# Gates of a linear recurrent unit in chains of three, half-height products in pairs, and retention in chunks of 256 tokens

## The chip, the cores and the metric

The kernel runs on one core of one Trainium2 chip. The metric is the device time of one execution, in microseconds (us), as the median of repeated runs. The engines are PE (matrix products), DVE, ACT and POOL (elementwise work) and SP, which here only issues transfers. They run in parallel and wait for each other on semaphores.

## What is computed

Two decoder layers on 1024 tokens of width 1024, in float32. The first layer's mixer is retention, the second's a gated linear recurrence (RG-LRU); each is followed by a dense SwiGLU. What the change touches is this:

```python
def step(state, inp):                      # retention, chunk by chunk, 4 heads, dk 256, dv 512
    qi, ki, vi = inp
    scores = jnp.einsum('bhqd,bhkd->bhqk', qi, ki) * intra[None]
    o_inner = jnp.einsum('bhqk,bhkv->bhqv', scores, vi)
    o_cross = jnp.einsum('bhqd,bhdv->bhqv', qi, state) * q_decay[None, :, :, None]
    new_state = state * chunk_decay[None, :, None, None] + jnp.einsum(
        'bhkd,bhkv->bhdv', ki * k_decay[None, :, :, None], vi)
    return new_state, o_inner + o_cross
...
# RG-LRU, width 1536 in 8 blocks of 192
r = jax.nn.sigmoid(jnp.einsum('bsnc,ncd->bsnd', ub, w_r) + b_r).reshape(B, S, LRU_WIDTH)
i = jax.nn.sigmoid(jnp.einsum('bsnc,ncd->bsnd', ub, w_i) + b_i).reshape(B, S, LRU_WIDTH)
log_a = (-LRU_C * jax.nn.softplus(-lam.astype(jnp.float32))) * r.astype(jnp.float32)
a = jnp.exp(log_a)
b = jnp.sqrt(-jnp.expm1(2.0 * log_a)) * (i * u).astype(jnp.float32)
...
y = hs.astype(h.dtype) * jax.nn.gelu(gate)   # hs: the scan of h = a*h + b over the tokens
return y @ w_out
```

The result does not depend on the length of a chunk, as long as the decays are kept.

## The kernel before

Every float32 operand of a product is held as two rounded parts, upper and lower, so a product takes three instructions on PE (helper `three`, lines 770 to 777: upper x upper at L773, the other two at L776 and L777). ACT (or POOL, for weights) makes the upper part, DVE (or POOL) the lower one by a subtraction. The order on each engine is the order of the code of that engine; nothing is scheduled. PSUM has 8 banks of 512 columns. Each use of a bank has a running number, an event; PE counts filled events in `psum_full`, and the engine that reads one last counts it in `psum_free`. `free(e)` makes PE wait until event e - 8, the last user of the same bank, is released, and `psum_free` is one counter, so every earlier event must be released too.

**Retention**, four heads in turn. PE makes q and k (pair 0 and pair 1 in `head` of DVE, which rotates them, L2009 to L2025, and splits them, L2030), the gate branch g, the scores (`SCORES`: for each key block of 128 tokens the queries that see it, in chunks of `CHUNK` = 4 blocks, 512 tokens), the turned keys (L966, L967, by an identity), and the values v. Then come `values(s)` for each of 8 blocks of 128 tokens and `state_sum`, the sum of k times v over the first chunk, in banks 6 and 7; ACT rounds the state (L1500), DVE splits it (L2069), and the later chunk's blocks multiply q with it. `o_turns` turns the gated output for the product with w_out.

**RG-LRU**, four groups of 3 tiles of 128 channels, which are two blocks of 192. Per group PE makes the u branch and the gate branch (`lru_into`, twice 3 tiles of 48 products), the output products of the group before (`lru_outof`), and the gate products (`lru_gates`). There an item is one tile and one half of the tokens, and has two banks, r and i. `MEETS` says which of the three 128-channel blocks of u a tile needs: tile 0 needs 0 and 1, tile 1 all three, tile 2 needs 1 and 2. The block 1 for tiles 0 and 2 is used only in half of its rows; the rest of the weights is zero. Seven blocks times two gates times three instructions are 42 per half.

The chain behind it, per pair of items, is `gate_chain` on ACT and DVE: sigmoid of r (L1777) and i (L1782), u times i on DVE (`gated`, L2405, which releases both banks), tanh (L1791) and exp (L1795) of r, square root (L1801), then on DVE in `scans` two multiplies (L2413, L2417), the scan (L2422) and the product with the other branch (L2429), and at last `y_split` (L2434). ACT loads a table when it goes from sigmoid and tanh to exp, and to the square root, and back. The function `meanwhile` puts adds of output products to the residual (`add`, L1998) between the steps of the last group.

In the last group the gates stand in the middle of the output products of the group before: s = 0 to 3 of the first half of columns, the gates, s = 4 to 7, and then the second half of columns (`lru_outof` with nh = 1, 72 products), whose k = 0 round takes one bank after the other: s = 4 needs the bank that the first half's s = 4 was added from. Behind it comes the last group's own output (`out_by_halves`, 16.3 us for a half), which needs y.

## Time and profile before

| | us |
|---|---|
| median of 3 runs | 2703.74 (2703.36 to 2703.92) |
| the profiled execution | 2702.78 |
| its span in the trace | 2701.0 |
| PE busy | 2672.0 (99%) |
| DVE busy | 1273.9 (47%) |
| ACT busy | 831.3 (31%) |
| POOL busy | 1267.7 (47%) |

The times of single instructions below are from the one profiled execution. A busy time on PE is that of one product from its first column to its last result, and neighbours overlap, so the distance from start to start is what a product takes of PE. Retention lies between 16 and 876 us, the first SwiGLU behind it, RG-LRU between some 1550 and 2027 us, and the second SwiGLU to the end.

### The profile page before, as it was taken

The numbers are of one execution on the slowest core, as the hardware profiler recorded it, in microseconds if no ns is written. First come the engines' busy times: TensorE is split into PE (matmuls) and PEld (weight loads), VectorE is DVE, ScalarE is ACT, GpSimd is POOL, SyncE is SP. The second block draws the span as 40 slices with busy tenths as digits, with TensorE's granted clock in tenths as the row PEclk, the third lists the DMA queues.
The fourth block names the chain that finished last, engine by engine and source line by source line (L and its number), as shares of the span: only waits on it lengthen the run. The fifth ranks groups of instructions, "written<-read, shape, count | busy, mean of one in ns | idle before, by whom it ended". The sixth has DMA issues, their size and how long they took to land.

```text
span 2701.0 us, 35201 instructions
## 1 busy us (share of the span) xinstructions
PE 2672.0 (99%) x12017; PEld 2213.0 (82%) x12017; DVE 1273.9 (47%) x1719; ACT 831.3 (31%) x1388; POOL 1267.7 (47%) x1208
## 2 busy tenths in 40 slices
PE   8999999999999999999999999999999999999998
PEld 6888888888888788888888788888887888888887
DVE  8333322323334854444444447365688444444444
ACT  4120120120124533333333515234365222222224
POOL 4324323323423455655555454363454556655555
PEclk9999999999999999999999999999999999999999
DMA  4101102111111111111121021111111111111212
GB/s 143 44 28 63 44 28 63 47 32 59 48 36 44 51 51 54 47 47 54 53 64 51 27 60 44 36 55 40 44 55 47 55 54 47 47 47 55 69 50 83
DMA packets 173768, 139.29 MB, mean 52 GB/s; under 512 B 9200, under 2 KB 143472, under 8 KB 173680
## 3 DMA queue, kind: packets, MB, share of 16 engines
q1 hardware_dynamic: 171584, 133.46, 16.2%
q10 hardware_dynamic: 2096, 4.62, 0.5%
q8 instruction: 59, 0.97, 0.1%
q14 instruction: 29, 0.24, 0.0%
HBM read 132.81 MB, written 5.24 MB: 51 GB/s over the span
## 4 chain that ended last, share of the span: by engine, by line
PE 95%; DVE 3%; ACT 1%; issue 1%; DMA 0%; SPq 0%; DVEq 0%
PE ps L773 31%; PE ps L777 31%; PE ps L776 31%; DVE f_h_lo L2144 1%; PE ps L1085 0%; PE ps L1009 0%; PE ps L849 0%; PE ps L911 0%; DMA residual<-in_x 0%; DVE gate_buf L2082 0%; DVE f_h_lo L2133 0%; DVE h_sum_a L2133 0%; DVE gate_buf L2222 0%; ACT f_h_hi L1581 0%; DVE h_sum_a L2158 0%
## 5 line engine op out<-in xcount | busy, mean ns | idle before, releaser
L602 POOL TENSOR_TENSOR f_w_lo<-f_raw,f_w_hi 128x512 fp32r<-128x512 f32 x270 | 357.5, 1326 | 449.6 <-ACT f_w_hi L1532 364.6
L773 PE MATMUL ps<-f_h_hi,f_w_hi 128*128 128x512 f32 x1232 | 481.1, 390 | 3.6 <-DVE f_h_lo L2144 2.3
L777 PE MATMUL ps<-f_h_hi,f_w_lo 128*128 128x512 f32 x1232 | 479.5, 389 | 0.0
L776 PE MATMUL ps<-f_h_lo,f_w_hi 128*128 128x512 f32 x1232 | 479.4, 389 | 0.0
L560 POOL TENSOR_TENSOR small<-w_raw 128x1 f32<-128x1 f32 x200 | 59.5, 297 | 804.6 <-PE ps L773 794.1
L2333 DVE TENSOR_TENSOR residual<-ps,residual 128x512 f32<-128x512 f32 x352 | 239.4, 691 | 170.5 <-PE ps L777 170.4
L773 PEld LDWEIGHTS ps<-f_h_hi,f_w_hi 128*128 128x128 f32 x1232 | 231.2, 188 | 57.2 <-issue 4.4
L1532 ACT ACTIVATE f_w_hi<-f_raw 128x512 fp32r<-128x512 f32 x246 | 155.1, 631 | 382.9 <-PE ps L777 382.8
L777 PEld LDWEIGHTS ps<-f_h_hi,f_w_lo 128*128 128x128 f32 x1232 | 231.3, 188 | 48.3
L776 PEld LDWEIGHTS ps<-f_h_lo,f_w_hi 128*128 128x128 f32 x1232 | 231.3, 188 | 47.2
L773 PE MATMUL ps<-f_w_hi,f_act_hi 128*128 128x512 f32 x688 | 267.8, 389 | 0.0
L776 PE MATMUL ps<-f_w_lo,f_act_hi 128*128 128x512 f32 x688 | 267.6, 389 | 0.0
L777 PE MATMUL ps<-f_w_hi,f_act_lo 128*128 128x512 f32 x688 | 267.6, 389 | 0.0
L571 POOL TENSOR_TENSOR w_lo<-w_raw,w_hi 128x512 fp32r<-128x512 f32 x190 | 259.1, 1364 | 15.2
L773 PE MATMUL ps<-h_hi,w_hi 128*128 128x512 f32 x632 | 247.5, 392 | 0.0
L777 PE MATMUL ps<-h_hi,w_lo 128*128 128x512 f32 x632 | 246.0, 389 | 0.0
L776 PE MATMUL ps<-h_lo,w_hi 128*128 128x512 f32 x632 | 246.0, 389 | 0.0
L602 POOL TENSOR_TENSOR f_w_lo<-f_sum,f_w_hi 128x512 fp32r<-128x512 f32 x124 | 180.4, 1455 | 124.1 <-ACT f_w_hi L1532 124.1
L773 PE MATMUL ps<-w_hi,h_hi 128*128 128x512 f32 x528 | 205.7, 390 | 0.4 <-DVE gate_buf L2021 0.4
L776 PE MATMUL ps<-w_lo,h_hi 128*128 128x512 f32 x528 | 205.5, 389 | 0.0
L777 PE MATMUL ps<-w_hi,h_lo 128*128 128x512 f32 x528 | 205.5, 389 | 0.0
L2288 DVE TENSOR_TENSOR gate_buf<-ps,gate_buf 128x512 f32<-128x512 f32 x120 | 82.8, 690 | 235.1 <-PE ps L777 235.0
(305 smaller groups left out, 4643.8 us busy)
## 6 DMA issues: line engine op xcount, KB each, us to landing
f_raw<-in_ffn_w_gu SPq DMA_DIRECT2D x176, 256.0 KB, 3.3
w_raw<-in_ret_w_in SPq DMA_DIRECT2D x96, 256.0 KB, 2.8
f_raw<-in_ffn_w_down SPq DMA_DIRECT2D x88, 256.0 KB, 2.8
w_raw<-in_lru_w_in SPq DMA_DIRECT2D x48, 256.0 KB, 2.9
w_raw<-in_ret_w_out SPq DMA_DIRECT2D x32, 256.0 KB, 2.6
w_raw<-in_lru_w_out SPq DMA_DIRECT2D x24, 256.0 KB, 2.6
residual<-in_x SPq DMA_DIRECT2D x8, 512.0 KB, 7.2
out_y<-residual SPq DMA_DIRECT2D x7, 512.0 KB, 2.6
```

What stands on the lines that cost most here:

```text
L560: nc.gpsimd.tensor_tensor(small[:, 62:63], col, col, ALU.subtract)
L571: nc.gpsimd.tensor_tensor(lo, raw[:, cut], hi.bitcast(F32), ALU.subtract).then_inc(w_ready, 1)
L602: nc.gpsimd.tensor_tensor(lo, src, hi.bitcast(F32), ALU.subtract).then_inc(f_wready, 1)
L773: m = nc.tensor.matmul(o, l_hi, r_hi, start=start, stop=False, skip_group_check=onto)
L776: nc.tensor.matmul(o, l_hi, r_lo, start=False, stop=False, skip_group_check=onto)
L777: return nc.tensor.matmul(o, l_lo, r_hi, start=False, stop=stop, skip_group_check=onto)
L1532: nc.scalar.activation(f_unit(j, last)[0], src, ACT.Copy).then_inc(f_whi, 1)
L2144: TT(H_lo[:, h_cut(form, k)], src[:, t_cut(k)], H_hi[:, h_cut(form, k)].bitcast(F32), ALU.subtract).then_inc(hn_dve, 1)
L2288: TT(t, f_bank(u, p), t, ALU.add).then_inc(f_ev, 1)
L2333: TT(X[:, c], ps[:, b * BANK:(b + 1) * BANK], X[:, c], ALU.add).then_inc(f_ev, 1)
```

## The change

Retention works in four chunks of 256 tokens: per chunk 128 and 256 columns of scores, turned keys for three chunks, and three states, each summed on top of the one before in the same banks (`state_sum(i)`, with waits for the split of the last). The queries of tokens 256 to 511 are copied a second time (`query_tile`), since v takes the place of the first copy.

The gate products run in another order (tile 1 first), and the six of block 1 for tiles 0 and 2 are issued on 64 rows each, in turn. The chain takes three items at a time, with more buffers. In the last group the first three items' chain takes item 3's sigmoids first (`early` = 1), and s = 4 to 7 of the output are made in two pairs.

```diff
-CHUNK = 4
...
-SCORES = [pieces for c in (0, CHUNK) for pieces in ([(c, 512)], [(c + 3, 128), (c + 1, 384)], [(c + 2, 256)])]
...
-MEETS = [(0, 1), (0, 1, 2), (1, 2)]
+CHUNK, N_CHUNKS = 2, 4
...
+SCORES = [(1, P), (0, 2 * P)]
+SCORE_N = 3 * P
...
+GATE_TILES = (1, 0, 2)
...
-        r_buf = (t(0), r3(6), dk[:, 0:512], spare[0])
+        r_buf = (t(0), r3(6), dk[:, 0:512], spare[0], behind[0][:], behind[1][:])
         i_buf = (t(1), spare[1], spare[2])
-        s_buf = (r3(7), t(2))
+        s_buf = (r3(7), t(2), behind[2][:])
...
+                        k_h, k_l = qk_at(1, d, i // 2)
+                        for c in range(CHUNK):
+                            q = (i % 2 * CHUNK + c) * P
+                            cut, o = slice(q, q + P), bank(J_K + i, (d * CHUNK + c) * P, P)
+                            nc.tensor.matmul(o, k_h[:, cut], ident_r[:], start=True, stop=False)
+                            m = nc.tensor.matmul(o, k_l[:, cut], ident_r[:], start=False, stop=True)
+                    m.then_inc(psum_full, 1 if i < N_CHUNKS - 2 else 2)
                 for k in range(KT):
                     cols_unit(16 + k, ub + 16 + k, k, KT, h_hi, h_lo, k * S, J_V, base)
...
+                def state_sum(i):
...
+                            pe.wait_ge(st_ready, 6 * h + 2 * i - 2 + d + 1)
...
-                            cut, v = slice(c * P, (c + 1) * P), slice(c * 512, (c + 1) * 512)
-                            m = three(bank(J_O + 6 + d), k_h[:, cut], k_l[:, cut], a_hi[:, v], a_lo[:, v],
-                                      c == 0, c == CHUNK - 1)
+                            k_h, k_l = k_turned(i, P, (d * CHUNK + c) * P)
+                            b = i * CHUNK + c
+                            v = slice(b * 512, (b + 1) * 512)
+                            m = three(bank(J_O + 6 + d), k_h, k_l, a_hi[:, v], a_lo[:, v],
+                                      i == 0 and c == 0, c == CHUNK - 1, onto=i > 0)
                         m.then_inc(st_full, 1)
-                pe.wait_ge(s_ready, h * len(SCORES) + len(SCORES))
+                pe.wait_ge(s_ready, h * N_CHUNKS + N_CHUNKS)
                 def values(s):
-                    late = s >= CHUNK
...
+                        m.then_inc(psum_full, 1)
+                def from_state(s):
+                    for d in range(2):
+                        pe.wait_ge(st_ready, 6 * h + (s // CHUNK - 1) * 2 + d + 1)
+                        m = three(bank(J_O + s), *query(s, d), *state(d), False, d == 1)
...
+                state_sum(0)
+                for i in (1, 2):
+                    values(2 * i)
+                    values(2 * i + 1)
+                    from_state(2 * i)
+                    from_state(2 * i + 1)
+                    state_sum(i)
+                o_turns(range(4))
+                for s in (6, 7):
                     values(s)
-                state_sum()
-                for s in range(3, SB - 1):
-                    values(s)
-                o_turns(range(4))
-                values(SB - 1)
+                    from_state(s)
                 if last:
...
+                    def halves_meet():
+                        for m_i in range(2):
+                            a_w, a_wl, a_u, a_ul = operands(0, m_i, 1, slice(0, 64))
+                            b_w, b_wl, b_u, b_ul = operands(2, m_i, 1, slice(64, P))
+                            a, b = bank(event(0, m_i)), bank(event(2, m_i))
+                            nc.tensor.matmul(a, a_w, a_u, start=False, stop=False)
+                            nc.tensor.matmul(b, b_w, b_u, start=False, stop=False)
+                            nc.tensor.matmul(a, a_w, a_ul, start=False, stop=False)
+                            nc.tensor.matmul(b, b_w, b_ul, start=False, stop=False)
+                            nc.tensor.matmul(a, a_wl, a_u, start=False, stop=True)
+                            m = nc.tensor.matmul(b, b_wl, b_u, start=False, stop=True)
...
+                        m.then_inc(psum_full, 4)
...
+                    if hf == 0:
+                        pe.wait_ge(u_ready, len(U_PIECES) * g + 2)
+                    meets(0, 0, True, False)
+                    meets(1, 0, True, False)
+                    meets(1, 1, False, False)
+                    pe.wait_ge(u_ready, len(U_PIECES) * g + 3 + hf)
+                    meets(1, 2, False, True)
+                    meets(2, 2, True, False)
+                    halves_meet()
...
-            for first in (0, 4):
+            for first, n in ((0, 4), (4, 2), (6, 2)):
...
-                    for s in range(first, first + 4):
+                    for s in range(first, first + n):
...
-                        .then_inc(qk_rounded, 1)
+                    src = (t(0), t(1), t(2), r3(7))[i % 4]
+                    nc.scalar.activation(qk_at(pair, d, hf)[0], src, ACT.Copy).then_inc(qk_rounded, 1)
+                    if pair == 0 and hf == 0:
+                        nc.scalar.activation(query_tile(d)[0], src[:, 256:512], ACT.Copy).then_inc(q2_rounded, 1)
...
                 def tanh_exp(items):
                     for i in items:
-                        if i >= 2:
-                            act.wait_ge(l_scan, 6 * g + i - 1)
...
+                            act.wait_ge(psum_free, base + e0 + 2 * (GT + early) + 2)
...
-                gates(4)
-                gates(5)
-                tanh_exp((2, 3))
-                roots((2, 3))
-                tanh_exp((4, 5))
-                y_round((2, 3))
-                roots((4, 5))
-                y_round((4, 5))
+                for i in range(GT + early):
+                    gates(i)
+                tanh_exp((0, 1, 2))
+                roots((0, 1, 2))
+                for i in range(GT + early, 2 * GT):
+                    gates(i)
+                tanh_exp((3, 4, 5))
+                y_round((0, 1, 2))
+                roots((3, 4, 5))
+                y_round((3, 4, 5))
...
-                split_state()
-                gate_o((3,))
-                gate_o((4,))
+                gate_o((0, 1))
+                split_state(0)
+                gate_o((2, 3))
+                split_state(1)
                 norm_o(0)
-                gate_o((5, 6))
+                gate_o((4, 5))
+                split_state(2)
                 o_turned_lower(range(4))
-                gate_o((7,))
+                gate_o((6, 7))
                 norm_o(1)
...
                     for j, i in enumerate(items):
                         dve.wait_ge(dve_step, first + j + 1)
-                        step.up(TT(uc[:, cut(i)], uc[:, cut(i)], s_buf[i % 2], ALU.mult))
+                        step.up(TT(uc[:, cut(i)], uc[:, cut(i)], s_buf[i % 3], ALU.mult))
+                    amid()
                     for j, i in enumerate(items):
-                        dve.wait_ge(dve_step, first + j + 3)
-                        tile, hf = i % GT, i // GT
+                        dve.wait_ge(dve_step, first + len(items) + j + 1)
...
                         start = uc[:, tile * S + 511:tile * S + 512] if hf else 0.0
-                        k = nc.vector.tensor_tensor_scan(uc[:, cut(i)], r_buf[i % 4], uc[:, cut(i)], start,
+                        k = nc.vector.tensor_tensor_scan(uc[:, cut(i)], r_buf[i], uc[:, cut(i)], start,
...
                 TS(gc_gate[:, 0:3], gc_gate[:, 21:24], -2.0, None, ALU.mult).then_inc(gc_ready, 1)
-                gated((0, 1))
-                scans((0, 1), amid=lambda: gated((2,)))
-                gated((3,))
-                y_split((0, 1))
-                gated((4, 5))
+                gated(range(GT + early))
+                scans((0, 1, 2), amid=lambda: gated(range(GT + early, 2 * GT)))
+                y_split((0, 1, 2))
                 meanwhile(0, range(4, SB))
-                scans((2, 3))
-                y_split((2, 3))
-                scans((4, 5), lambda: meanwhile(1, range(SB)))
-                y_split((4, 5))
+                scans((3, 4, 5), lambda: meanwhile(1, range(SB)))
+                y_split((3, 4, 5))
             per_turn = 1 + 3 * 3 + 1 + 6 * 2
```

On PE in the last group, behind the products of tile 1 and 2: `h_hi`, `h_lo` are the parts of u, `wri_hi`, `wri_lo` those of the gate weights. Before, in the first half of the tokens:

```order
L773 MATMUL ps<-h_hi,wri_hi 128x512 [waits psum_free]
L776 MATMUL ps<-h_lo,wri_hi 128x512
L777 MATMUL ps<-h_hi,wri_lo 128x512
L773 MATMUL ps<-h_hi,wri_hi 128x512
L776 MATMUL ps<-h_lo,wri_hi 128x512
L777 MATMUL ps<-h_hi,wri_lo 128x512
L773 MATMUL ps<-h_hi,wri_hi 128x512 [waits u_ready,psum_free]
L776 MATMUL ps<-h_lo,wri_hi 128x512
L777 MATMUL ps<-h_hi,wri_lo 128x512
L773 MATMUL ps<-h_hi,wri_hi 128x512
L776 MATMUL ps<-h_lo,wri_hi 128x512
L777 MATMUL ps<-h_hi,wri_lo 128x512
```

After, from the same half, the first twelve of block 1 for tiles 0 and 2:

```order
L1323 MATMUL ps<-h_hi,wri_hi 128x512
L1324 MATMUL ps<-h_hi,wri_hi 128x512
L1325 MATMUL ps<-h_lo,wri_hi 128x512
L1326 MATMUL ps<-h_lo,wri_hi 128x512
L1327 MATMUL ps<-h_hi,wri_lo 128x512
L1328 MATMUL ps<-h_hi,wri_lo 128x512
L1323 MATMUL ps<-h_hi,wri_hi 128x512
L1324 MATMUL ps<-h_hi,wri_hi 128x512
L1325 MATMUL ps<-h_lo,wri_hi 128x512
L1326 MATMUL ps<-h_lo,wri_hi 128x512
L1327 MATMUL ps<-h_hi,wri_lo 128x512
L1328 MATMUL ps<-h_hi,wri_lo 128x512
```

Twelve instructions on 128 rows become twelve that stand alternately on rows 0 to 63 (L1323, L1325, L1327) and 64 to 127, behind all others of the half.

On DVE in the last group, from the first products of y on (`gate_buf` from the scan `uc`) to the next adds to the residual. Before:

```order
L2429 TENSOR_TENSOR gate_buf<-uc,gate_buf 128x512 [waits l_scan] x2
L2405 TENSOR_TENSOR uc<-uc,tmp 128x512 [waits i_sig]
L2434 TENSOR_TENSOR h_lo<-gate_buf,h_hi 128x512 [waits y_rounded] x2
L2405 TENSOR_TENSOR uc<-uc,xn 128x512 [waits i_sig] x2
L1998 TENSOR_TENSOR residual<-ps,residual 128x512 [waits psum_full] x4
```

After, the same stretch; the multiplies and the scans ahead of it are shown too:

```order
L2492 TENSOR_TENSOR uc<-uc,gate_buf 128x512 [waits dve_step]
L2492 TENSOR_TENSOR uc<-uc,tmp 128x512 [waits dve_step]
L2492 TENSOR_TENSOR uc<-uc,lru_gate 128x512 [waits dve_step]
L2480 TENSOR_TENSOR uc<-uc,xn 128x512 [waits i_sig] x2
L2498 SCALAR_TENSOR_TENSOR uc<-tmp,uc 128x512 [waits dve_step]
L2498 SCALAR_TENSOR_TENSOR uc<-gate_buf,uc 128x512 [waits dve_step]
L2498 SCALAR_TENSOR_TENSOR uc<-mask,uc 128x512 [waits dve_step]
L2503 TENSOR_TENSOR gate_buf<-uc,gate_buf 128x512 [waits l_scan] x3
L2508 TENSOR_TENSOR h_lo<-gate_buf,h_hi 128x512 [waits y_rounded] x3
L2065 TENSOR_TENSOR residual<-ps,residual 128x512 [waits psum_full] x4
```

The four adds, which stood behind `y_split` of two items and two `gated`, now stand behind the scans, products and `y_split` of three items.

## Rows read from the trace of the kernel before

**Rows 1.** The page: busy time by engine, and the last chain by engine.
```profile
PE 2672.0 (99%) x12017; PEld 2213.0 (82%) x12017; DVE 1273.9 (47%) x1719; ACT 831.3 (31%) x1388; POOL 1267.7 (47%) x1208
...
PE 95%; DVE 3%; ACT 1%; issue 1%; DMA 0%; SPq 0%; DVEq 0%
```

**Rows 2.** Waits of PE, longest first: total, times, longest, in us.
```profile
PE ps L874 <- DMA scratch<-in_lru_lambda: 9.6, 1, 9.6
```

**Rows 3.** Line 773, last group's gates: count, min/median/max ns, first, last start.
```profile
L773 PE MATMUL ps<-h_hi,wri_hi x28: 389/389/389, 1946.6 to 1965.0; 128*128 128x512 f32 x28
```

**Rows 4.** Timeline of PE, scores of head 0: start us, us, engine.
```profile
109.69 0.39 PE L773 MATMUL ps<-a_hi 128*128 128x512 f32 x1
...
111.22 0.27 PE L777 MATMUL ps<-a_hi,a_lo 128*128 128x128 f32 x1
111.33 0.27 PE L773 MATMUL ps<-a_hi 128*128 128x128 f32 x1
...
112.90 0.28 PE L776 MATMUL ps<-a_lo,a_hi 128*128 128x256 f32 x1
113.02 0.28 PE L777 MATMUL ps<-a_hi,a_lo 128*128 128x256 f32 x1
...
117.32 0.22 PE L966 MATMUL ps<-ident_r,a_hi 128*128 128x128 f32 x1
...
119.06 0.44 PE L773 MATMUL ps<-w_hi,h_hi 128*128 128x512 f32 x1
```

**Rows 5.** Timelines of DVE and of ACT, states and values of head 0.
```profile
158.97 5.37 DVE L2062 SCALAR_TENSOR_TENSOR a_lo<-ps,gam,a_hi 128x512 fp32r<-128x512 f32 x8 [38.28 <-ACT a_hi L1481]
...
169.67 0.60 ACT L1500 ACTIVATE b_hi<-ps 128x512 fp32r<-128x512 f32 x1 [1.94 <-PE ps L777]
...
170.30 0.69 DVE L2069 TENSOR_TENSOR b_lo<-ps,b_hi 128x512 fp32r<-128x512 f32 x1 [1.78 <-ACT b_hi L1500]
```

**Rows 6.** Timeline of DVE: a 256-wide instruction of the scores.
```profile
114.19 0.42 DVE L2047 TENSOR_TENSOR tmp<-ps,mask 128x256 f32<-128x256 f32 x1
```

**Rows 7.** Timelines of DVE and PE ahead of the k pair.
```profile
64.97 0.69 DVE L2009 TENSOR_TENSOR tmp<-ps,gate_buf 128x512 f32<-128x512 f32 x1
...
70.76 0.50 PE L773 MATMUL ps<-w_hi,h_hi 128*128 128x512 f32 x1 [0.38 <-DVE gate_buf L2021]
...
267.82 0.69 DVE L2009 TENSOR_TENSOR tmp<-ps,gate_buf 128x512 f32<-128x512 f32 x1 [1.44 <-PE ps L777]
```

**Rows 8.** Timelines of DVE and ACT ahead of the gates of group 2.
```profile
1852.28 3.07 DVE L1998 TENSOR_TENSOR residual<-ps,residual 128x512 f32<-128x512 f32 x5
...
1858.73 1.28 ACT L1777 ACT_TABLE_LOAD   x1 [3.16 <-DVE gc_gate L2439]
```

**Rows 9.** Timeline of ACT, gate chain of the last group.
```profile
1948.22 1.28 ACT L1777 ACT_TABLE_LOAD   x1 [5.60 <-PE ps L777]
1949.51 0.69 ACT L1777 ACTIVATE tmp<-ps,gc_gate 128x512 f32<-128x512 f32 x1
1950.10 0.68 ACT L1782 ACTIVATE tmp<-ps,gc_gate 128x512 f32<-128x512 f32 x1
...
1956.84 0.73 ACT L1795 ACTIVATE tmp<-tmp,gc_gate 128x512 f32<-128x512 f32 x1
...
1959.50 0.63 ACT L1801 ACTIVATE gate_buf<-gate_buf 128x512 f32<-128x512 f32 x1
```

**Rows 10.** Timeline of PE behind the gates of the last group.
```profile
1967.43 0.50 PE L773 MATMUL ps<-w_hi,a_hi 128*128 128x512 f32 x1 [0.26 <-DVE uc L2405]
...
1977.11 0.39 PE L773 MATMUL ps<-w_hi,a_hi 128*128 128x512 f32 x1
```

**Rows 11.** Timeline of DVE, gate chain of the last group.
```profile
1962.66 1.22 DVE L2422 TENSOR_TENSOR_SCAN uc<-tmp,uc 128x512 f32<-128x512 f32 x1
...
1972.55 2.73 DVE L1998 TENSOR_TENSOR residual<-ps,residual 128x512 f32<-128x512 f32 x4 [1.79 <-PE ps L777]
...
1976.29 1.78 DVE L2413 SCALAR_TENSOR_TENSOR tmp<-xn,tmp 128x512 f32<-128x512 f32 x1
```

More of the change, by code:

```diff
@@ L217, in build @@
               for kb in (123, 127, 131, 135)]
+        behind = [over(kb, f"lru_gate{kb}", 512) for kb in (159, 161, 163)]
         f_hi, f_lo = over(44, "f_w_hi", RING * 512, F32R), over(50, "f_w_lo", RING * 512, F32R)
@@ L1496, in head @@
                                          accum_out=ssq[:, s:s + 1]).then_inc(o_sq, 1)
-                    if s == 2:
-                        for d in range(2):
-                            act.wait_ge(st_full, 2 * h + d + 1)
-                            nc.scalar.activation(state(d)[0], bank(J_O + 6 + d), ACT.Copy).then_inc(st_rounded, 1)
-                    if s == 6:
-                        o_turned_upper(range(4))
                     if s % 4 == 3:
@@ L1506, in head @@
                                              scale=1.0 / DV).then_inc(o_root, 1)
+                    if s in (1, 3, 5):
+                        for d in range(2):
+                            act.wait_ge(st_full, 6 * h + s - 1 + d + 1)
+                            nc.scalar.activation(state(d)[0], bank(J_O + 6 + d), ACT.Copy).then_inc(st_rounded, 1)
+                    if s == 5:
+                        o_turned_upper(range(4))
                 o_turned_upper(range(4, SB))
```

204 lines of the change are left out of this document (102 added, 102 removed).

## The prediction, before the changed kernel ran

> **What bounds the kernel now.** I read the shares of the span first: PE is busy 99% of it, and the chain that ended last runs on PE for 95% [rows 1]. The list of waits then says how little PE waits: the longest is 9.6 us before its first instruction, which this change does not touch [rows 2], and the others are far smaller. So an edit is worth what it takes out of PE's stream of products, minus the waits that it creates. The price of a product comes from start to start, not from its busy time of 389 ns, which overlaps its neighbour: 27 triples start between 1946.6 and 1965.0, 0.681 us a triple, so a **slot** is 0.227 us for 512 columns [rows 3]. Narrow ones are not proportional: 128 columns start 0.11 apart and 256 columns 0.12 [rows 4]. A product of 128 columns should stream in a quarter of the slot, so 0.11 is what the load of its 128x128 weights costs. That floor prices half of this change.
>
> **Scores and turned keys** (each of 4 heads). Before, the 48 score products take 109.69 to 117.32, 7.63 us, and the 16 turns 117.32 to 119.06, 1.74 us or 0.109 each [rows 4]. After, the scores are 24 products of 128 and 24 of 256 columns: 24 x 0.111 + 24 x 0.119 = 5.52 us, and 24 turns are 2.61 us. Gain 9.37 - 8.13 = 1.24 a head, **-5.0 us**. By columns alone it would be 5120 fewer, 2.27 us a head, but the floor of 0.11 takes half.
>
> **States and values.** Before: 28 triples of values and 8 of the state; after: 12 on the diagonal, 12 from a state, 12 for three states. 108 slots both times, so **0**. What is new is three passes PE -> ACT -> DVE -> PE. Nearest rows: the state's copy on ACT takes 0.60, the split on DVE 0.69 and starts 0.03 after it [rows 5]. With the product's end and the two blocks in front on both engines, the second half of state 0 is ready 1.7 us after state_sum(0) ends, and PE has 9 products of values(2), values(3) and 3 of the first half in front, 2.7 us. The later two have 12 slots and the 16 transposes. state_sum(0) now starts after 9 slots instead of 18, at 162.67 + 2.04 = 164.7, and waits for the last of the value splits, which ends at 158.97 + 5.37 = 164.34 [rows 5]. Covered by 0.3 us; were the cover gone, it is 0.3 to 1 us a head. I take 0.
>
> **The extra halves of q.** Two 256-wide splits on DVE (busy 0.42 [rows 6], 0.33 from start to start if they overlap by 0.09 as the 0.69-long adds below do) and two copies on ACT stand before the k pair. In heads 1 to 3 DVE idles 1.44 us there [rows 7], so they are hidden. In head 0 it has a backlog (no idle at 64.97) and PE already waits 0.38 for its result at 70.76 [rows 7]: all of it shows, **+0.7 us**. Retention: -4.3.
>
> **The gate products.** Per half and group 42 products before, all with full slots, half of the rows of 12 of them zeros (tile 0 and tile 2 against the middle block). After, these 12 stand as 6 pairs on rows 0 to 63 and 64 to 127. No row shows fewer than 128 rows. Low bound for a pair: two weight loads, 2 x 0.111 = 0.222; high bound: two slots, 0.454. The halves share no row and no PSUM bank, only the loader, so I take one slot, 0.227: 6 slots less, 1.36 us a half, 2.72 a group. The first and last product of such a block meet full-height ones. If one must be out before the next begins, that is 0.389 - 0.227 = 0.16 at each side, plus one uncovered weight load of 0.11: 0 to 0.9 us a block, I take 0.45.
>
> The Trainium skill (TensorE: Matmul & The Clock Gate, Part 3: Packing small matmuls) says that products on different row groups run side by side, starting 4 ns apart, with 3.07x measured for four; by it a pair is a slot plus 4 ns, the value that I take, and no row here shows it. Against the change speaks the Trainium skill (TensorEngine Tiling (Array Packing), Key Properties): a change of tiling mode drains the engine. By it the low end of 0 for a block would fall away; it does not change the value taken.
>
> Two new waits stand in this stage. (1) The first triple of a group now writes the second item's bank, and needs 3 and 4 of the second adds instead of 1 and 2. In the loop's groups the adds start at 1852.28, 0.6 apart, the third ends at 1854.17, and the gates start at 1854.13 [rows 8]: 0.1 each. (2) Item 0 is now tile 1 and is full only after 24 products. In the last group: 23 slots + 0.39 + 0.1 = 5.7 us after the stage's start T0. Then ACT loads a table, 1.28, and makes two sigmoids, 0.6 apart and 0.69 long [rows 9], and DVE multiplies, 0.69: the banks are free at T0 + 9.1, while PE is there at 8.2 to 8.6. Group 0 has the same order, table load included; in groups 1 and 2 ACT was held until 1858.73 + 1.28 = 1860.0 anyhow [rows 8], T0 + 5.9, and frees at about T0 + 8.0, in time. So group 0 takes 9.15 + 8.16 + 0.45 = 17.75 against 19.05, -1.3; groups 1 and 2 take 0.1 + 16.33 + 0.9 = 17.35, -1.7 each. **-4.7 us**. Behind these groups stand 65 us of input products, so the longer chain is free; it needs item 3 released 28 us after T0, and the sum below puts that at 23.
>
> **The last group** has only 20 blocks of output products behind it, and here I expect the loss. Before, PE begins s=4 of the last turn's second half at 1977.11, T0 + 30.5 [rows 10]; its bank needs the DVE add of s=4, which came at 1972.55 after a wait for PE [rows 11], so free. After, that add stands behind y_split of three items. From T0: second half starts 9.15, item 3 is full 14.85, its sigmoids to 16.1, three tanh to 17.9, table 1.28, three exp (0.73 long) to 21.2, table to 22.5, three roots (0.63 long) to 24.2, table to 25.5, sigmoids of items 4 and 5 to 27.9 [rows 9]. DVE: three STT from 23.3, three multiplies to 26.95, gated(4) to 27.6, gated(5) to 28.7, three scans (1.22 long, 1.14 apart [rows 11]) to 32.1, three multiplies to 34.1, y_split of three to 35.6, the first add to 36.3. DVE has hardly an idle microsecond in it, and single instructions stretch from 0.69 to 1.78 while POOL splits weights [rows 11]; POOL has three units to do there, so + 1.0. PE also waits for item 4 first (27.65 against 25.9), inside the same stretch. PE starts s=4 at T0 + 37.3, 6.8 later than before. The three items' second turn then makes DVE some 1.5 us later at the next norm, of which PE sees perhaps 0.5, since it waits there little. **+7.3 us** instead of -2.7.
>
> **Sum.** -5.0 + 0.7 - 4.7 + 7.3 = -1.7 us. The profiled execution is 2702.78 (span 2701.0 and 1.8 around), so 2701.1 for it; the median of runs is 1.0 above it: 2703.74 - 1.7 = **2702.0 us**.
>
> **Rivals.**
> A, as summed, with ends: blocks at 0 or 0.9 instead of 0.45 (-2.3 / +2.7 in the six that show), stretch by POOL 0 to 3. 2697 to 2706, chance 0.50.
> B, the last chain does not hold PE: the DVE order lets the add through in time, or POOL and ACT are quicker than the rows, and the last group gains like group 0. For it: the change splits PE's last four blocks in two pairs, which takes a wait away (0.26 idle at 1967.43 [rows 10]). Against: the order of DVE puts y_split ahead of the add. -5.0 + 0.7 - 4.7 - 1.3 = -10.3: 2693.4. Chance 0.15.
> C, slower: pairs do not overlap, that is the change doesn't do what it says on PE. Each half then keeps 42 slots and adds 0.45. It decides at the price of a pair: over about 0.38 us. For it: every product in the trace, however narrow, has a slot of its own; against: nothing but the loader is shared. -4.3, groups 0 to 2 + 2.9, the last one 7.3 + 0.8, since item 3 is full that much later: +6.7, 2710.4. Chance 0.20.
> D, between A and B: the stall is there but half as long, because parts of the chain overlap more: -5, 2698.5, chance 0.15.
>
> **How the numbers follow.** A change of this kernel can be told from none at about 0.2%, 5.4 us. Faster by more is B, a part of D, a thin end of A: 0.22. Slower by more is most of C and the end of A: 0.20. The rest, 0.58, is within. The range takes A and D and reaches to C: 2695 to 2710, with the middle of B left out; the likeliest case alone is 2697 to 2706.
>
> **What would show it.** In the profile after: score products of a head in 5.5 us; pairs on the gate stage that start 0.227 apart as pairs (or 0.227 each, which is C); in group 0 a wait of PE for DVE's product of uc at T0 + 9; in the last group a wait of 1 to 2 us for item 4 and one of 5 to 8 us for the residual add before s=4 of the second half, the largest new wait of PE; in head 0 a wait of 1.1 us where 0.38 was. No wait in from_state. If the wait for the residual add is missing, or starts of the two halves of a pair are a slot apart, the prediction is wrong.

## The result, and the profile after

The changed kernel takes **2707.33 us** (median of 20 runs, 2706.36 to 2709.57), the kernel before 2703.61 us on the same chips (20 runs, 2702.88 to 2704.11): a ratio of 1.0014, 95% interval 1.0008 to 1.0021. The time lies inside the range of 2695 to 2710 and within the 0.2% that I called no change, but the sign of the forecast was wrong: -1.7 us was expected and about +3.7 came. The profiled run of the changed kernel is 2706.43 us long (span 2704.6), 3.65 more than the 2702.78 of before. This difference is taken apart below, by where PE stands in both traces.

The page of the changed kernel, busy time by engine and the last chain, beside [rows 1]:

```profile
PE 2665.1 (99%) x12049; PEld 2202.0 (81%) x12049; DVE 1291.4 (48%) x1731; ACT 828.2 (31%) x1400; POOL 1268.2 (47%) x1208
...
PE 90%; DVE 7%; ACT 2%; issue 1%; DMA 0%; SPq 0%; DVEq 0%; ACTq 0%
```

PE has 7 us less to do and yet the kernel is longer, and DVE's share of the last chain has gone from 3% to 7%. PE's list of waits (total, times, longest) names the new holders; the first row answers to [rows 2]:

```profile
PE ps L896 <- DMA scratch<-in_lru_lambda: 9.5, 1, 9.5
PE ps L795 <- DVE residual L2065: 6.1, 2, 6.0
...
PE ps L795 <- DVE uc L2480: 2.9, 1, 2.9
...
PE ps L795 <- DVE gate_buf L2088: 0.4, 1, 0.4
PE ps L795 <- DVE gate_buf L2083: 0.3, 1, 0.3
```

The two long ones are the two that the prediction placed in the last group: 2.9 us for the product on DVE (line 2480) that frees item 4's banks, and 6.0 us for the residual add (line 2065) that stands behind y_split. The timeline of PE around them (start us, length us, engine, line; a bracket is idle time and its releaser), beside [rows 10]:

```profile
1967.19 0.47 PE L795 MATMUL ps<-w_hi,a_hi 128*128 128x512 f32 x1 [2.91 <-DVE uc L2480]
...
1968.35 0.63 PE L798 MATMUL ps<-w_lo,a_hi 128*128 128x512 f32 x1
1968.78 0.63 PE L799 MATMUL ps<-w_hi,a_lo 128*128 128x512 f32 x1
...
1977.75 0.80 PE L795 MATMUL ps<-w_hi,a_hi 128*128 128x512 f32 x1 [5.99 <-DVE residual L2065]
...
1981.71 0.39 PE L795 MATMUL ps<-w_hi,a_hi 128*128 128x512 f32 x1
1981.94 0.39 PE L798 MATMUL ps<-w_lo,a_hi 128*128 128x512 f32 x1
```

Look at the distance between starts. 1968.35 to 1968.78 is 0.43 us and 1981.71 to 1981.94 is 0.23: behind each of the two waits PE runs for a while at half its pace (behind the first one only from its fourth product on). The stretches with the granted clock (length, busy time and count of PE, PEld, DVE, ACT, POOL, then the clock, the DMA share and GB/s) say why:

```profile
1965.00:1975.00 10.00, 4.58 (x12) 3.28 (x12) 10.00 (x10) 6.55 (x10) 7.26 (x6) 0.82 0.25 79
1975.00:1980.00 5.00, 2.25 (x5) 1.82 (x6) 5.00 (x9) 3.91 (x6) 0.00 (x0) 0.50 0.00 2
1980.00:1985.00 5.00, 5.00 (x20) 4.06 (x19) 1.29 (x3) 0.00 (x0) 1.99 (x3) 0.84 0.01 3
1985.00:1990.00 5.00, 5.00 (x24) 4.14 (x23) 1.29 (x2) 0.00 (x0) 1.58 (x4) 1.00 0.15 52
```

The granted clock is 0.50 between 1975 and 1980, that is 1.2 GHz instead of 2.4. From 1977.75 to 1981.71 PE starts 9 products in 3.96 us, where nine slots at full clock are 2.04: **1.9 us** lost after the wait was over. Nothing in the prediction has a price for that, though the trace of the kernel before holds an example. At the norm ahead of RG-LRU, PE waits 2.93 us for DVE, and the granted clock of the next 3.5 us is 0.63 in the mean:

```profile
1545.10 5.11 PE L911 MATMUL ps<-ident,xn 128*128 128x128 f32 x23 [2.93 <-DVE xn L1895]
...
1545.00:1548.50 3.50, 3.33 (x13) 2.51 (x14) 2.32 (x6) 2.86 (x6) 0.00 (x0) 0.63 0.00 0
```

The Trainium skill (TensorE: Matmul & The Clock Gate, Part 1: The HAM clock gate) says that half rate is the engine's resting state and that activity releases it; the trace agrees, with 0.50 during and behind a wait of 6 us and 1.00 once the products run again.

The rest is a comparison of the two traces at the same product, later minus earlier position of PE:

| place | before | after | difference | forecast there |
| --- | --- | --- | --- | --- |
| scores of head 0 begin | 109.69 | 110.39 | +0.70 | +0.7 |
| v products of head 0 begin | 119.06 | 118.53 | -0.53 | -0.54 |
| gates of group 0 begin | 1620.2 | 1616.3 | -3.9 | -4.3 |
| gates of the last group begin (T0) | 1946.6 | 1938.7 | -7.9 | -9.0 |
| s=4 of nh=1 in the last turn begins | 1977.11 | 1977.75 | +0.6 | -2.2 |
| first w, h product of the last output | 1990.71 | 1993.27 | +2.6 | -2.2 |
| last FFN stage | 2671.5 | 2675.1 | +3.6 | -1.7 |

So the path gains 7.9 us up to the last group and loses 11.5 in it and at the norm behind it.

### The profile page after: what moved, and what is told of

Read it like the earlier page. It is cut to its first block, busy times and chain, and to the rows that moved or that the text cites. A ratio compares the mean times of both kernels' runs of the same rounds, so it can differ in the third digit from the quotient of the medians.

```text
span 2704.6 us, 35316 instructions
## 1 busy us (share of the span) xinstructions
PE 2665.1 (99%) x12049; PEld 2202.0 (81%) x12049; DVE 1291.4 (48%) x1731; ACT 828.2 (31%) x1400; POOL 1268.2 (47%) x1208
## 4 chain that ended last, share of the span: by engine, by line
PE 90%; DVE 7%; ACT 2%; issue 1%; DMA 0%; SPq 0%; DVEq 0%; ACTq 0%
PE ps L795 29%; PE ps L799 29%; PE ps L798 29%; DVE uc L2498 1%; DVE f_h_lo L2218 1%; DVE gate_buf L2503 1%; PE ps L1124 0%; DVE uc L2492 0%; PE ps L1042 0%; DVE uc L2454 0%; DVE residual L2065 0%; DMA residual<-in_x 0%; ACT L1871 0%; DVE gate_buf L2155 0%; PE ps L933 0%
```

## Experiments

All ratios are to the kernel before, run beside each on the same chip. Its median there lay between 2703.24 and 2703.50 (2703.61 beside the changed kernel), so a difference between two kernels that ran on different chips can be off by 0.4 us. Positions in single profiles carry up to 1 us of their own: the kernel of experiment 3, unchanged up to there, begins the gates of group 0 at 1621.1, the kernel before at 1620.2.

**1. Retention alone, and the gates alone.** The first kernel takes from the diff only what concerns retention, the second only what concerns the gates. One place of each edit is shown.

```diff
-CHUNK = 4
+CHUNK, N_CHUNKS = 2, 4
```

> The kernel before with the four chunks of retention and nothing of the gates changed. In the profile of the changed kernel PE stands 3.9 us earlier than before from the end of retention up to the gates of group 0, so my theory is 3.9 us less than before (about 2699.8 beside 2703.6), with each head's scores and turned keys at 8.14 us instead of 9.37 and a wait of 0.7 to 0.8 us for the extra halves of q in head 0. The rival: the gain is given back behind the gates, because some later stage waits for DVE or POOL and not for PE; then it is under 2 us less (2701.8 or more).

Measured: 2698.86 us beside 2703.24, ratio 0.9985 (0.9976 to 0.9994): 4.4 us less. Its gain is kept to the end: in the trace the last stage of the FFN begins at 2668.2 instead of 2671.5.

```diff
-MEETS = [(0, 1), (0, 1, 2), (1, 2)]
+GATE_TILES = (1, 0, 2)
```

> The kernel before with the new gate stage (pairs on 64 rows, chain of three, last four blocks in two pairs) and the old retention. Theory: the two parts are independent, so this is the changed kernel plus 3.9 us: 7.5 us over before, about 2711.1, with PE's waits of 2.9 us (item 4) and 6.0 us (residual add) in the last group and some 17 products at 0.43 us from start to start behind them. The rival, that the 3.7 us of the changed kernel come from retention and gates meeting (a queue or a buffer they share): then this one is within 4 us of before.

Measured: 2711.78 us, ratio 1.0030 (1.0019 to 1.0041): 8.5 us more. The waits are there again without the new retention:

```profile
PE ps L776 <- DVE residual L2027: 6.4, 2, 6.2
...
PE ps L776 <- DVE uc L2435: 2.9, 1, 2.9
```

-4.4 and +8.5 add up to +4.1, where the whole change gave +3.7. The two parts don't meet; the loss is all in the gates.

**2. The four residual adds earlier.** In the last group DVE does them ahead of the scans instead of behind y_split.

```diff
-                scans((0, 1, 2), amid=lambda: gated(range(GT + early, 2 * GT)))
-                y_split((0, 1, 2))
-                meanwhile(0, range(4, SB))
+                def amid():
+                    gated(range(GT + early, 2 * GT))
+                    meanwhile(0, range(4, SB))
+                scans((0, 1, 2), amid=amid)
+                y_split((0, 1, 2))
```

> The changed kernel with one edit on DVE, in the last group's chain: the four residual adds that PE waits for stand right behind the products that free items 4 and 5, ahead of the scans, and not behind y_split. Theory: the wait of 6.0 us goes, and with it the 9 products at the lower granted clock that follow it (9 x 0.2 = 1.8 us), while the wait of 2.9 us for item 4 and its 8 slow products stay: 7.8 us less than the changed kernel, about 2699.5. Rival 1, the clock's low stretch does not hang on the wait: 6.0 less, 2701.3. Rival 2, the chain as a whole is too long and the wait only moves (the scans and y come 2.4 us later, PE then waits for them or for the adds of the second half): less than 4 us less, 2703 or more.

Measured: 2699.59 us, ratio 0.9987 (0.9978 to 0.9996), 7.7 us less than the changed kernel (7.4 if each is taken from the kernel before beside it) and as expected. The wait of 6.0 is gone, the one for item 4 stays at 2.9, and the slow products stand behind that one alone; in PE's timeline

```profile
1967.92 0.76 PE L795 MATMUL ps<-w_hi,a_hi 128*128 128x512 f32 x1 [2.91 <-DVE uc L2480]
```

and the stretch behind it, with the clock:

```profile
1968.00:1972.00 4.00, 4.00 (x10) 3.13 (x11) 4.00 (x6) 3.97 (x6) 3.34 (x4) 0.50 0.19 67
```

Ten products in 4 us, at a clock of 0.50. There are 13 slow ones in all, where 8 stood behind the same wait in the changed kernel. The second wait did not simply cut those short: the granted clock was back at 0.99 between 1971.7 and 1974.9, with PE standing still. Why the slow stretch is longer here is not shown.

**3. The same late adds in the kernel before.** Nothing of the change is in this kernel; the adds go behind the second scans.

```diff
-                meanwhile(0, range(4, SB))
                 scans((2, 3))
+                meanwhile(0, range(4, SB))
```

> The kernel before, with nothing of the change, and one edit on DVE in the last group: the four residual adds stand behind the scans of the second pair of items instead of ahead of them. DVE does those scans until about 1983.5 and PE wants the first add at 1977.1, so PE waits about 6 us. Theory: what costs beyond the wait is the granted clock, which falls after a wait of that length whatever the kernel: 6.3 + some 9 to 13 products at 0.43 instead of 0.227 (1.8 to 2.6) + 0.5 at the next norm, 8.6 to 9.4 us over before, about 2712.5. Rival: the slow products belong to the new gate stage (its pairs on half the rows, or its longer chain on DVE and ACT), not to the wait: then 6.3 to 7 us over before, about 2710.

Measured: 2711.83 us, ratio 1.0032 (1.0020 to 1.0044), 8.5 us more for a wait of 6.2, just under the 8.6 to 9.4 of the theory and above the 6.3 to 7 of the rival; in the list of PE's waits

```profile
PE ps L773 <- DVE residual L1998: 6.2, 1, 6.2
```

and behind it the stretch from 1984 to 1988, at 0.50 again:

```profile
1984.00:1988.00 4.00, 3.69 (x9) 2.95 (x10) 3.71 (x7) 3.92 (x6) 0.00 (x0) 0.50 0.00 2
```

The slow products belong to the long wait and not to the pairs or the chain of three: here there is neither.

**4. All sigmoids first.** ACT makes all six items' sigmoids before the first tanh, so that both waits should go.

```diff
-            gate_chain(GROUPS - 1, base, L_RI_LAST, h_hi, 1)
+            gate_chain(GROUPS - 1, base, L_RI_LAST, h_hi, 3)
...
-            gate_chain(GROUPS - 1, h_hi, h_lo, group_before_out, 1)
+            gate_chain(GROUPS - 1, h_hi, h_lo, group_before_out, 3)
...
+                meanwhile(0, range(4, SB))
                 scans((0, 1, 2), amid=lambda: gated(range(GT + early, 2 * GT)))
                 y_split((0, 1, 2))
-                meanwhile(0, range(4, SB))
-                scans((3, 4, 5), lambda: meanwhile(1, range(SB)))
+                meanwhile(1, range(SB))
+                scans((3, 4, 5))
```

(ACT's tanh of the second three items then waits for the scans of the first, since the roots' buffers are theirs.)

> The changed kernel with another order in the last group's chain: ACT makes the sigmoids of all six items before the first tanh, DVE multiplies all six and does the first four residual adds before the scans, and the eight adds of the second half stand ahead of the second three items. ACT's chain then starts some 4.7 us later and saves one table load. Theory: both waits of PE go, 2.9 and 6.0, and the 17 slow products, 3.4 to 3.7 us: 12.3 to 12.6 less than the changed kernel, about 2694.9. Rival: the later chain makes y of the second three items late; by my count it is ready between 1992 and 1996 on the trace's clock, and PE wants it at 1997. If POOL stretches DVE by more than that, PE waits there and the time is 2697 to 2700.

Measured: 2699.26 us, ratio 0.9986 (0.9977 to 0.9995), in the range of the rival. Both waits went, and a third came: the adds of the second half are late now.

```profile
1984.12 0.67 PE L795 MATMUL ps<-w_hi,h_hi 128*128 128x512 f32 x1 [2.64 <-DVE residual L2067]
1984.58 0.63 PE L798 MATMUL ps<-w_lo,h_hi 128*128 128x512 f32 x1
```

The theory was 4 us too low. I had looked for the lateness at y of the second three items; it showed one place earlier, and again with slow products behind it.

**5. Both kinds of work interleaved.** ACT's order is that of the changed kernel, DVE frees items 4 and 5 between its multiplies. Not shown in the cut: the four adds stand ahead of the scans, and four of the eight later adds ahead of the second three items.

```diff
                     for j, i in enumerate(items):
                         dve.wait_ge(dve_step, first + j + 1)
                         step.up(TT(uc[:, cut(i)], uc[:, cut(i)], s_buf[i % 3], ALU.mult))
+                        if early and i < 2:
+                            gated((4 + i,))
```

> The changed kernel with another order on DVE in the last group: the product that frees item 4 stands behind the first multiply, the one that frees item 5 behind the second, the four residual adds behind the third and ahead of the scans, and the first four of the eight later adds ahead of the second three items. ACT's order is that of the changed kernel. Theory: PE's wait for item 4 falls from 2.9 us to about 1 (its sigmoid is ready some 3.3 us ahead of where DVE used it), the wait of 6.0 us goes, and a wait of about 1 us is too short to bring the granted clock down, since the waits of 0.3 to 0.7 us of the changed kernel do not: 2699.6 - 1.9 - 2.6 (13 products at 0.43 instead of 0.227 in the run with only the adds moved) = 2695.1. Rival 1: any wait brings the clock down; then 2697.5. Rival 2: DVE is by now what bounds the last group, since it has no idle time between the first scan and the next norm; PE then waits at the norm for what it gained, and the time is 2697 to 2699.

Measured: 2698.80 us, ratio 0.9984 (0.9975 to 0.9993): rival 2. PE's waits in the last group, from its timeline:

```profile
1965.60 0.47 PE L795 MATMUL ps<-w_hi,a_hi 128*128 128x512 f32 x1 [1.30 <-DVE uc L2482]
...
2000.59 0.47 PE L795 MATMUL ps<-w_hi,h_hi 128*128 128x512 f32 x1 [0.91 <-DVE residual L2067]
2010.91 1.28 PE L1124 MATMUL ps<-ident,gate_buf 128*128 128x128 f32 x10 [1.89 <-DVE gate_buf L2196]
```

and the stretch behind the first of them:

```profile
1968.00:1972.00 4.00, 3.37 (x15) 2.45 (x14) 4.00 (x6) 2.56 (x3) 2.67 (x4) 1.00 0.24 74
```

A wait of 1.3 us left the clock at 1.00. But PE, which was 7.5 us ahead of before at the first w, h product, is 4.3 ahead at the norm's first transpose: it waits for DVE there. To test that DVE itself is the limit, the next kernel is the same with six of DVE's instructions of the second three items on 64 columns; their other 448 columns are left out of the computation.

```diff
-                        step.up(STT(s_buf[i % 3], r_buf[i], 1.0, s_buf[i % 3], ALU.add, ALU.mult))
+                        n = 64 if early and i >= 3 else 512
+                        step.up(STT(s_buf[i % 3][:, 0:n], r_buf[i][:, 0:n], 1.0, s_buf[i % 3][:, 0:n],
+                                    ALU.add, ALU.mult))
```

> The kernel interleaved, with less work on DVE in the last group: the three products with the root and the three multiplies of the second three items are made on 64 of the 512 columns, so that the rest of these columns is left out of the computation. That takes 6 x (0.60 - 0.15) = some 2.7 us, and up to 5 with the stretches, from DVE between 1982 and 1993. Theory: DVE bounds the last group by then; PE's waits of 0.9 (residual) and 1.9 us (next norm) go or shrink, 2.0 to 2.8 us less than interleaved: about 2696.4. Rival: PE's late norm has another cause (the adds wait for PE's own products, a round trip that no DVE work fills): then no difference, 2698.8.

Measured: 2696.32 us, 2.5 us less, as expected; the wait of 0.9 is gone from the list and that of 1.9 is down to 0.5. DVE bounds the last group once the two long waits are away.

**6. The last group as before.** Retention and groups 0 to 2 as changed, the last group's products, chain and adds taken from the kernel before.

```diff
-                    lru_gates(GROUPS - 1, base, L_RI_LAST, h_hi, h_lo)
+                    lru_gates_all(GROUPS - 1, base, L_RI_LAST, h_hi, h_lo)
...
-            gate_chain(GROUPS - 1, h_hi, h_lo, group_before_out, 1)
+            gate_chain_two(GROUPS - 1, h_hi, h_lo, IN_ORDER, group_before_out)
```

> The changed kernel, but the last group's gates, their chain on ACT and DVE and the four blocks of products behind them are those of the kernel before (42 full-height products a half, items in pairs, tile order 0, 1, 2); retention and groups 0 to 2 as changed. Theory: the changed kernel's last group starts its gates 7.9 us earlier than before, and with the old chain everything behind keeps that distance: 2703.3 - 7.9 = 2695.4, the fastest so far, with PE's waits there as before (0.3 us, and none of 2.9 or 6.0). Rival: the last group's DVE work does not move with the gates, since POOL's weight splits that stretch it fall elsewhere; then 1 to 3 us are lost at the next norm, 2696.5 to 2698.5.

Measured: **2695.09 us** beside 2703.50, ratio 0.9970 (0.9959 to 0.9981). It is the fastest of all, 12 us under the changed kernel. PE's only wait at the gates is that of [rows 10], and the last stage of the FFN begins 8.0 us earlier than before, at 2663.5:

```profile
PE ps L797 <- DVE uc L2609: 0.2, 1, 0.2
```

and the last stage's products (count, ns min/median/max, first and last start):

```profile
L797 PE MATMUL ps<-f_last_hi,f_act_hi x16: 389/389/389, 2663.5 to 2683.9; 128*128 128x512 f32 x16
```

**7. Pairs without the chain of three.** As experiment 6, and groups 0 to 2 keep the pairs but take the old chain of two items at a time.

```diff
-                gate_chain(g, a_hi, a_lo)
+                gate_chain_two(g, a_hi, a_lo, GATE_TILES)
```

> As the kernel before it in this set (last group as in the kernel before the change), and in groups 0 to 2 the new products (pairs, tile order 1, 0, 2) but the old chain of two items at a time on ACT and DVE. What it tells: whether the 0.3 to 0.55 us that PE loses behind each of the groups 0 to 2, waiting for DVE's convolution of the next group, come from the chain of three. Theory: yes; DVE is 3.5 us later there with three at a time, with two it is not: 1.4 us less than with the chain of three, about 2694.0. Rival: the loss comes from PE being 2 us ahead with the pairs, and stays: no difference between the two, within 0.3 us.

Measured: 2707.66 us, ratio 1.0018 (1.0009 to 1.0027), 12.6 us slower than experiment 6 where I had expected 1.4 faster. In PE's list of waits there are four now, three of them long,

```profile
PE ps L797 <- DVE uc L2609: 9.1, 4, 3.0
```

and the stretch behind the first of them:

```profile
1636.00:1640.00 4.00, 3.82 (x11) 3.04 (x12) 4.00 (x7) 2.20 (x4) 3.18 (x2) 0.64 0.02 4
```

The banks that PE wants right behind the gates are those of item 2. With three items at a time its product on DVE is among the first three; with two at a time it stands behind the first scan. PE waits about 3.0 us in each of the three groups, and slow products follow. In the kernel before the same order did no harm: in its last group that product ended at T0 + 17.9, and PE was there at T0 + 19.0. Here, in group 0, it ends 20.0 us behind the start of the gates and PE is there after 17.1, since the pairs shorten the stage and tile 1, which now comes first, is full later. So the chain of three earns what the pairs save in groups 0 to 2. That the same chain is what costs in the last one, with pairs or without, the next experiment shows.

**8. What a pair costs.** Two kernels with other products in the same places. In the first each pair is two full-height products, rows of zeros included.

```diff
-                            nc.tensor.matmul(a, a_w, a_u, start=False, stop=False)
-                            nc.tensor.matmul(b, b_w, b_u, start=False, stop=False)
...
+                            for tile in (0, 2):
+                                m = three(bank(event(tile, m_i)), *operands(tile, m_i, 1), False, True)
```

> The changed kernel with the pairs on 64 rows replaced by 12 full-height products a half, rows of zeros included, in the same place and order; all else as in the changed kernel. Theory: a pair costs one slot of 0.227 and each of the 8 blocks 0.39 for entering and leaving, so this adds 12 x 0.227 - 2 x 0.39 = 1.94 us a group, 7.8 in all, about 2715. Rival: what a pair saves is hidden behind DVE's chain anyway (groups 0 to 2 are followed by waits of 0.3 us for DVE that were not there before, and in the last group PE waits for the residual add whatever it does): then only 3 to 5 us more, 2710 to 2712.

Measured: 2712.40 us, ratio 1.0034 (1.0021 to 1.0046), 5.1 us over the changed kernel, at the rival's upper end. The gates take 1.9 us a group more, what a pair at one slot makes; of this 1.5 is left at the start of each next group and 0.6 in the last, since PE waits for DVE there whatever it saves. From T0 to the last FFN stage this kernel takes 737.0 us, the changed one 736.4, the kernel before 724.9 and experiment 6 724.8: the loss of the last group comes from the chain and the order on DVE that goes with it, not from the pairs.

```profile
PE ps L795 <- DVE residual L2058: 8.2, 2, 8.0
...
PE ps L795 <- DVE uc L2473: 1.6, 1, 1.6
```

In the second kernel the order within a block is a, a, a, b, b, b.

```diff
                             nc.tensor.matmul(a, a_w, a_u, start=False, stop=False)
-                            nc.tensor.matmul(b, b_w, b_u, start=False, stop=False)
                             nc.tensor.matmul(a, a_w, a_ul, start=False, stop=False)
-                            nc.tensor.matmul(b, b_w, b_ul, start=False, stop=False)
                             nc.tensor.matmul(a, a_wl, a_u, start=False, stop=True)
+                            nc.tensor.matmul(b, b_w, b_u, start=False, stop=False)
+                            nc.tensor.matmul(b, b_w, b_ul, start=False, stop=False)
```

> The changed kernel with the six products of a block in the order a, a, a, b, b, b instead of a, b, a, b, a, b (a on rows 0 to 63, b on rows 64 to 127). Theory: PE takes products in order, and two overlap only where neighbours lie on different rows; there are then 3 such places in a block of 12 instead of 6 pairs, 9 slots instead of 6: 0.68 us a block, 5.4 us in all where nothing hides it, some 3 to 5.4 us over the changed kernel (2710.5 to 2712.7). Rival: the pairs overlap in any order because the queue is looked through ahead: no difference. Rival 2: no overlap at all at such a place: 12 slots, up to 10.9 us more.

Measured: 2707.36 us, ratio 1.0015 (1.0006 to 1.0024): no difference from the changed kernel, so my theory fell. From the last product ahead of a block to the second behind it, all eight blocks take 2.24 to 2.25 us, as in the changed kernel. Its timeline of PE, where lines 1323 to 1325 are a and 1326 to 1328 are b:

```profile
1622.80 0.49 PE L1323 MATMUL ps<-a_hi,wri_hi 64*128 64x512 f32 x1
1622.81 0.49 PE L1326 MATMUL ps<-a_hi,wri_hi 64*128 64x512 f32 x1
1623.13 0.39 PE L1324 MATMUL ps<-a_lo,wri_hi 64*128 64x512 f32 x1
1623.14 0.39 PE L1327 MATMUL ps<-a_lo,wri_hi 64*128 64x512 f32 x1
```

The fourth product of the program starts 0.01 behind the first and 0.32 ahead of the second.

This trace holds one thing more. PE waits 2.92 us for item 4, as in the changed kernel, but no slow stretch follows: the granted clock is 1.00 from 1966 to 1970. The wait for the residual add is then 7.3 us instead of 6.0, and PE starts s=4 at T0 + 39.0 in both.

## Why the prediction was wrong

**Scores and turned keys: right.** After, beside [rows 4]:

```profile
110.39 0.22 PE L795 MATMUL ps<-a_hi 128*128 128x128 f32 x1
...
115.91 0.22 PE L990 MATMUL ps<-ident_r,a_hi 128*128 128x128 f32 x1
...
118.53 0.45 PE L795 MATMUL ps<-w_hi,h_hi 128*128 128x512 f32 x1
```

5.52 us for the scores and 2.62 for the turns, against 5.52 and 2.61. The floor of 0.11 us for a narrow product holds for the new shapes.

**Extra halves of q: right in the sum,** +0.70 at the scores of head 0. It came as two waits of 0.35 and 0.40 us (lines 2083 and 2088), where one of 1.1 was named. States and values: -0.53 before them and -0.55 behind them, no wait; right. With 0.3 us lost in one later head, retention gave 3.9 of the 4.3.

**Pairs: right.** A block in group 0:

```profile
1622.89 0.39 PE L799 MATMUL ps<-a_hi,wri_lo 128*128 128x512 f32 x1
1623.20 0.49 PE L1323 MATMUL ps<-a_hi,wri_hi 64*128 64x512 f32 x1
1623.21 0.49 PE L1324 MATMUL ps<-a_hi,wri_hi 64*128 64x512 f32 x1
1623.54 0.39 PE L1325 MATMUL ps<-a_lo,wri_hi 64*128 64x512 f32 x1
...
1623.77 0.39 PE L1327 MATMUL ps<-a_hi,wri_lo 64*128 64x512 f32 x1
...
1624.79 0.50 PE L795 MATMUL ps<-a_hi,wri_hi 128*128 128x512 f32 x1
1625.13 0.40 PE L798 MATMUL ps<-a_lo,wri_hi 128*128 128x512 f32 x1
```

The halves of a pair start 0.01 apart and pairs follow at 0.23. Entering the block costs 0.08 (1622.89 to 1623.20 less a slot) and 0.11 at the second pair, leaving it 0.09 and 0.11: 0.39 us in all, against 0.45. Rival C is out. The Trainium skill (TensorEngine Tiling (Array Packing), Key Properties) says that a change of tiling mode drains the engine; the trace agrees in so far as both ends of a block cost something, and does not tell how much of it is the drain.

**Groups 0 to 2: -4.0 for -4.7.** Group 0's gates take 17.1 us (1616.3 to 1633.4), 0.7 less than summed: the wait at T0 + 9 that I had for group 0 did not come. I had counted 24 products until ACT can begin on item 0; its first sigmoid needs 21, so all is 0.7 earlier and DVE's product ends at T0 + 8.4 (in the last group 1946.40 + 0.69, below). But some 1.4 us is lost again in waits that the sum did not have: 0.4 behind groups 0 and 1 and 0.2 behind group 2, each 44 us after the gates, where I had called the longer chain free, and the rest in smaller ones at and in the gates of groups 1 and 2. The consumer that I checked was item 3; the one that showed is the next group's convolution on DVE, which frees the banks of the input products:

```profile
1673.23 3.98 DVE L2454 SCALAR_TENSOR_TENSOR uc<-ps,gc_conv,uc 128x1023 f32<-128x1023 f32 x3
...
1677.34 0.49 PE L795 MATMUL ps<-h_hi,w_hi 128*128 128x512 f32 x1
```

**The last group: +11.5 for +7.3. This is the step that failed, and it turned the sign.** Both waits were named, with their places; for 1 to 2 and 5 to 8 us, 2.9 and 6.0 came. What the term of 7.3 lacked, in the order in which it shows:

```profile
1946.40 0.69 DVE L2480 TENSOR_TENSOR uc<-uc,tmp 128x512 f32<-128x512 f32 x1 [6.49 <-ACT tmp L1849]
...
1960.83 0.69 DVE L2488 SCALAR_TENSOR_TENSOR gate_buf<-tmp,gate_buf 128x512 f32<-128x512 f32 x1 [6.36 <-ACT gate_buf L1871]
...
1963.66 1.76 DVE L2492 TENSOR_TENSOR uc<-uc,tmp 128x512 f32<-128x512 f32 x1
...
1965.95 2.79 DVE L2480 TENSOR_TENSOR uc<-uc,xn 128x512 f32<-128x512 f32 x2
...
1971.27 2.23 DVE L2498 TENSOR_TENSOR_SCAN uc<-mask,uc 128x512 f32<-128x512 f32 x1
...
1977.02 2.47 DVE L2065 TENSOR_TENSOR residual<-ps,residual 128x512 f32<-128x512 f32 x4
```

- DVE's chain was longer. From the first instruction with the root to PE's start at 1977.75 it took 16.9 us, where 13.0 + 1.0 for POOL were summed. From start to start three multiplies took 3.3 us instead of 1.85, the two products behind them 2.7 instead of 1.75 and three scans 4.8 instead of 3.4. The chain began 1.2 us earlier than summed, which gave part of it back. s=4 of nh=1 started at T0 + 39.0 and not at T0 + 37.3: **1.7 us**. POOL splits weights without a pause from 1962.1 to 1972.4, and all the long instructions of DVE start between 1962.6 and 1971.3; before and behind, products and splits are at 0.66 to 0.69. The Trainium skill (SBUF — State Buffer, SBUF: two separate sides) has DVE, where it reads two operands from SBUF, and POOL lock each other out of a shared pair of ports; the coincidence is in the trace, the cause was not tested.
- The granted clock fell: **1.9 us** behind the wait of 6.0. The half-rate products behind the first wait cost nothing more, since they only shortened the second; the second kernel of experiment 8 had none there and started s=4 as late.
- At the norm **1.25 us** (from +2.56 at 1993.27 to +3.81 at its second group of products) instead of 0.5, as DVE's second turn of three was late too.

The miss is 1.7 + 1.9 + 0.75 = 4.4 us, of the 5.4 by which the sum of -1.7 missed the 3.65 of the trace; 0.4 is in retention and 0.7 in groups 0 to 2, and 0.2 was given back behind the norm. The rivals don't cover it: A had the stretching in its range and no term for the clock, and ended at 2706. That 2707.33 still lies in the range of 2695 to 2710 is luck: the range went that far for C, and C's mechanism, pairs that do not overlap, is not what happened. Experiments 2 and 3 show the wait and the clock to be the cause, with and without the change; experiments 5 and 6 show that the last group had no room for a chain of three even where those waits are taken away.

## What to carry to other kernels

A wait is not priced by its length alone: PE may run its next products at 1.2 GHz. Here that was 1.4 to 2.9 us on top of waits of 2.6 to 8.0 us, in all but one case of 2.9 us, and nothing on top of waits of 1.3 to 1.9 us. A change that pays in every turn of a loop need not pay in the last one, where the work that covered its latency has ended; keep the old order for the last turn and compare (12 us here). When a chain on another engine is made longer, list all that waits for its end, not only the first buffer that it frees.

## What was not expected of the hardware

- Half-height products on different rows ran side by side in both orders of the program that were tried within a block of six: a, a, a, b, b, b took the same time as a, b, a, b, a, b, and the fourth started 0.32 us ahead of the second. The Trainium skill (TensorE: Matmul & The Clock Gate, Part 3: Packing small matmuls) has matrix products start and end strictly in the order of the program; this trace does not agree, and the measurement decides.
- The clock level fell at waits of 2.6, 2.9, 3.0, 6.0, 6.2, 7.3 and 8.0 us (products 0.43 us apart, the granted clock down to 0.50) and stayed at 1.00 behind 1.3, 1.6, 1.7 and 1.9 us. A wait of 2.9 us was on either side: three kernels had slow products behind the one for item 4 (some 6, 8 and 13 of them), the kernel with a, a, a, b, b, b had none.
- Work that PE saves in front of a wait for DVE hardly shows: in the last group the pairs save 1.95 us, and 0.6 of it is left at the last FFN stage.
